# A recurrence in groups of 128 tokens: the block inverse on 32x32 tiles of TensorE, another order of VectorE's work, and two steps on GpSimd

## What is computed

```python
def step(S, inp):
    r_t, w_t, k_t, v_t, kk_t, a_t = inp
    sa = jnp.einsum('bhvk,bhk->bhv', S, -kk_t)
    S = (S * w_t[:, :, None, :]
         + sa[..., None] * (kk_t * a_t)[:, :, None, :]
         + v_t[..., None] * k_t[:, :, None, :])
    return S, jnp.einsum('bhvk,bhk->bhv', S, r_t)
_, o = lax.scan(step, S0, xs)
...
o = ((o - mean) * lax.rsqrt(var + GN_EPS)).reshape(B, T, W)
...
return (o * g.astype(jnp.float32)).astype(p.dtype)
```

## Time and profile before

| | us |
|---|---|
| median of 3 runs (lowest, highest) | 1324.94 (1324.16, 1328.39) |
| the profiled execution's own time | 1324.93 |
| its span, first to last instruction | 1323.0 |
| TensorE busy (share of the span) | 1275.8 (96%) |
| VectorE busy | 853.1 (64%) |
| ScalarE busy | 479.3 (36%) |
| GpSimd busy | 254.3 (19%) |
| mean granted TensorE clock | 0.994 of full speed |

### The profile page before, as it was taken

How to read it: one execution, slowest core, us unless ns; L and a number is a source line. 1 busy time by engine, 2 the same in 40 slices (tenths; PEclk the granted TensorE clock), 3 DMA queues, 4 the chain that set the end, 5 groups by cost and what they waited for, 6 DMA issues and landing times.

```text
span 1323.0 us, 18110 instructions
## 1 busy us (share of the span) xinstructions
PE 1275.8 (96%) x6973; PEld 1057.7 (80%) x6973; DVE 853.1 (64%) x1308; ACT 479.3 (36%) x847; POOL 254.3 (19%) x196
## 2 busy tenths in 40 slices
PE   7999999989899999999999999999999999999996
PEld 6888888655698888888878888888888888888885
DVE  6865623399778787744476656566777676546765
ACT  6100032488422232234363333333333334333334
POOL 0476600034300000000003331332233200000001
PEclk9999999999999999989999999999999999999998
DMA  5576532200322333333214123214544567766643
GB/s 222 173 246 232 207 121 92 104 2 17 80 71 71 75 103 94 115 123 127 80 48 127 52 93 96 83 62 159 175 141 162 191 222 293 250 210 209 210 140 135
DMA packets 117232, 179.05 MB, mean 135 GB/s; under 512 B 30368, under 2 KB 59040, under 8 KB 116896
## 3 DMA queue, kind: packets, MB, share of 16 engines
q1 hardware_dynamic: 117152, 177.96, 41.0%
HBM read 123.90 MB, written 53.49 MB: 134 GB/s over the span
## 4 chain that ended last, share of the span: by engine, by line
PE 88%; DVE 7%; issue 2%; DMA 2%; ACT 2%; POOL 0%; DVEq 0%; SPq 0%; ACTq 0%; POOLq 0%
PE bank L2317 28%; PE bank L369 21%; PE bank L2417 15%; PE bank L1400 4%; PE bank L474 2%; PE bank L383 2%; PE bank L1271 1%; PE bank L1527 1%; PE bank L1485 1%; PE bank L1479 1%; DVE scores L1178 1%; PE bank L992 1%; PE bank L1497 1%; PE bank L1514 1%; PE bank L1501 1%
## 5 line engine op out<-in xcount | busy, mean ns | idle before, releaser
L2317 PE MATMUL bank<-thi,ahi 128*128 128x512 f32 x320 | 124.5, 389 | 0.0
L2317 PE MATMUL bank<-tlo,ahi 128*128 128x512 f32 x320 | 124.5, 389 | 0.0
L2317 PE MATMUL bank<-thi,alo 128*128 128x512 f32 x320 | 124.5, 389 | 0.0
L2417 PE MATMUL bank<-ch,dwh 128*128 128x512 f32 x308 | 120.3, 391 | 0.6 <-DVE dwl L1995 0.6
L2417 PE MATMUL bank<-ch,dwl 128*128 128x512 f32 x308 | 119.9, 389 | 0.0
L2417 PE MATMUL bank<-cl,dwh 128*128 128x512 f32 x308 | 119.8, 389 | 0.0
L348 DVE TENSOR_TENSOR ring_wlo<-ring_raw,ring_whi 128x1024 fp32r<-128x1024 f32 x30 | 40.6, 1352 | 121.9 <-ACT ring_whi L342 121.9
L369 PE MATMUL bank<-hhi,ring_whi 128*128 128x512 f32 x288 | 114.4, 397 | 0.0
L369 PE MATMUL bank<-hhi,ring_wlo 128*128 128x512 f32 x288 | 112.2, 390 | 0.0
L369 PE MATMUL bank<-hlo,ring_whi 128*128 128x512 f32 x288 | 112.1, 389 | 0.0
L2317 PE MATMUL bank<-x1hi,ahi 128*128 128x512 f32 x240 | 93.4, 389 | 0.0
(11 more groups left out here) (336 smaller groups left out, 2862.2 us busy)
## 6 DMA issues: line engine op xcount, KB each, us to landing
hraw<-hid_scratch SPq DMA_DIRECT2D x12, 1024.0 KB, 5.7
hid_scratch<-hid SPq DMA_DIRECT2D x22, 512.0 KB, 6.1
hid_scratch<-rt SPq DMA_DIRECT2D x11, 1024.0 KB, 4.7
dwr<-down_sums SPq DMA_DIRECT2D x16, 704.0 KB, 4.2
ring_raw<-in_w_in SPq DMA_DIRECT2D x20, 512.0 KB, 4.3
raw_a<-in_w_gate_up SPq DMA_DIRECT2D x20, 512.0 KB, 4.4
raw_b<-in_w_gate_up SPq DMA_DIRECT2D x20, 512.0 KB, 5.2
dwr<-in_w_down SPq DMA_DIRECT2D x12, 704.0 KB, 4.1
```

The lines of the kernel that those rows point to most:

```text
L2317: mm = pe.matmul(b[:, :], w[:, k, :], m[:, k, :], start=opens and k == 0 and i == 0, stop=not (j, n) in parts and k == 3 and i == 2, skip_ ...
L2417: mm = pe.matmul(b[:, :], w[m % 2][:, k, :], a[:, k, :], start=opens and k == 0 and i == 0, stop=name not in PART2 and k == KF - 1 and i = ...
```

## The change

It touches the recurrence, and the end of stage 8.

- **Levels 1 and 2** become matmuls on 32x32 tiles of the array (`blocks_of`). Level 1 has 32 matmuls for `t1` (16 columns each), 32 for `y1` (32 columns) and 16 for `x1` (16 columns), which computes the change of `X` and takes the place of the transposes; level 2 has 16 for `t2` and 16 for `y2` (32 columns each). Those of `t1` and `y1` go through four tiles on the array's diagonal in turn, the others through two.
- **The tiles shrink**: `X` and `XT` hold 64 instead of 128 columns for each head, `Ts1` and `Ts2` hold 32. Each of the two loads in `scatter` becomes two loads of 64 partitions. `vtk` has two buffers, and its load moves ahead of `scatter`.
- **VectorE**: one multiplication (`first_corners`) and two additions (`first_updates`) are left of levels 1 and 2. `masked` b moves from the end of a group to the start of the next; `lanes` stands ahead of `prepare`; `Sn` stands ahead of `masked` k. The scaling of the mean goes into the instruction that makes `oc`, which now waits for the mix sum of the group before.
- **ScalarE** makes the copies of level 2 (`Ts2`, and two into `XT`), and copies `bt` and `kt` ahead of scaling `S`.
- **GpSimd** normalises (`on`) and adds to `mix`, except for the last group.
- **TensorE**: the product of the state for `R` stands first in a group, the products of `KB` stand between the steps of levels 1 and 2, and `bt` and `kt` around the close of the state. `busy` issues matmuls of 128x512 whose result is not used: four in group 0, three in group 7.
- **Stage 8**: the transposes of three quarters move to `k == 7`, and ScalarE squares those three quarters before the last one is there, in instructions of their own (`square_three`, then `square_last` on 128 columns).

The diff, cut. GpSimd and the copies in memory first:

```diff
-                sp.dma_start(X[:, :, :], bass.AP(d_i.tensor, P, [[2 * P, P], [8 * IMG2, H], [1, P]])).then_inc(s_xl, 16)
-                if t:
-                    C.result(sp, "U", t - 1)
-                sp.dma_start(XT[:, :, :], bass.AP(d_i.tensor, 0, [[2 * P, P], [8 * IMG2, H], [1, P]])).then_inc(s_xt, 16)
+                for m, o, done in ((X, P, s_xl), (XT, 0, s_xt)):
+                    if t and m is XT:
+                        C.result(sp, "U", t - 1)
+                    for q in range(2):
+                        sp.dma_start(m[q * HD:(q + 1) * HD, :, :],
+                                     bass.AP(d_i.tensor, o + q * (2 * P + 1) * HD, [[2 * P, HD], [8 * IMG2, H], [1, HD]])
+                                     ).then_inc(done, 16)
...
                     gather(t + 1)
+                    sp.wait_ge(s_vtk, 16 * t + 16)
+                    if t:
+                        C.result(sp, "S", t - 1)
+                    sp.dma_start(vtk_[(t + 1) % 2][:, :], v_dram[tok(t + 1), :]).then_inc(s_vtk, 16)
                     scatter(t + 1)
-                    C.result(sp, "S", t)
-                    sp.dma_start(vtk[:, :], v_dram[tok(t + 1), :]).then_inc(s_vtk, 16)
...
+                if t < NT - 1:
+                    pool.wait_ge(s_rstd, 2 * t + 2)
+                    pool.tensor_tensor(on[:, :, :], oc[:, :, :], rstd.unsqueeze(2).to_broadcast([P, H, HD]), ALU.mult
+                                       ).then_inc(s_on, 1)
+                    C.emptied(pool, "ot", t)
+                    pool.tensor_tensor(mix[:, 0:NP, tok(t)], oc[:, :, :].rearrange("p (a b) n -> p a (b n)", a=NP),
+                                       mix[:, 0:NP, tok(t)], ALU.add).then_inc(s_mix, 1)
```

TensorE's new functions, and the start of a group:

```diff
+            def blocks_of(b, count, lhs, rhs, groups):
+
+                n = len(groups) * H
+                for h in range(H):
+                    for g in groups:
+                        lo, ro = lhs(g, h), rhs(g, h)
+                        to = g[2]
+                        mm = pe.matmul(b[32 * to:32 * to + 32, h * count:(h + 1) * count] if len(ro.shape) == 2 else
+                                       b[32 * to:32 * to + 32, h * count:(h + 1) * count].rearrange("p (a w) -> p a w", a=2),
+                                       lo, ro, start=h == 0, stop=h == H - 1, skip_group_check=True)
...
+
+            FOUR = [(g, g % 2, g) for g in range(4)]
...
+                if n == 1:
+                    b = C.claim(pe, "t1", t)
+                    pe.wait_ge(s_xl, 32 * t + 32)
+                    C.done(blocks_of(b, 16, lambda g, h: NB[t % 2][rows(g[0]), h, 1, rows(g[0])],
+                                     lambda g, h: X[rows(g[0]), h, 32 * g[1]:32 * g[1] + 16], FOUR), "t1", t)
+                else:
+                    b = C.claim(pe, "t2", t)
+                    C.emptied(pe, "x1", t)
+                    C.done(blocks_of(b, 32, lambda g, h: NB[t % 2][rows(g[0]), h, 1, rows(g[2])],
+                                     lambda g, h: X[rows(g[0]), h, 0:32], [(0, 0, 1), (2, 0, 3)]), "t2", t)
...
+                C.emptied(pe, f"t{n}", t)
+                if n == 1:
+                    b = C.claim(pe, "y1", t)
+                    C.done(blocks_of(b, 32, lambda g, h: Ts1[rows(g[0]), h, :],
+                                     lambda g, h: XT[rows(g[0]), h, :].rearrange("p (a w) -> p a w", a=2)[:, :, 16:32], FOUR),
+                           "y1", t)
+                    b = C.claim(pe, "x1", t)
+                    C.done(blocks_of(b, 16, lambda g, h: XT[rows(g[0]), h, 0:32],
+                                     lambda g, h: Ts1[rows(g[0]), h, 0:16], [(0, 0, 0), (2, 0, 2)]), "x1", t)
+                else:
+                    C.emptied(pe, "y1", t)
+                    b = C.claim(pe, "y2", t)
+                    C.done(blocks_of(b, 32, lambda g, h: Ts2[rows(g[0]), h, :],
+                                     lambda g, h: XT[rows(g[0]), h, 32:64], [(1, 0, 0), (3, 0, 2)]), "y2", t)
+
+            def busy(b, n):
+                for _ in range(n):
+                    pe.matmul(b[:, :], ident, cst[:, 0:HALF], start=True, stop=True)
...
+                br = C.claim(pe, "R", t)
+                if t == 0:
+                    busy(br, 2)
+                else:
+                    pe.wait_ge(s_S, t)
+                of_state(br, alpha, True)
                 if t:
...
+                    corners(1, t)
                 pe.wait_ge(s_vtk, 16 * t + 16)
                 for g in range(4):
                     C.emptied(pe, f"k{g}", t)
...
+                products_of(br, 1, *range(H)).then_inc(s_r, 1)
...
-                              stop=False, skip_group_check=True)
+                if t == 0:
+                    corners(1, t)
+                    products_of(bo, 0, *range(4))
+                    busy(C.claim(pe, "S", t), 1)
+                pe.wait_ge(s_xt, 32 * t + 32)
+                updates(1, t)
+                if t == 0:
+                    busy(C.claim(pe, "S", t), 1)
+                else:
+                    products_of(bo, 0, *range(4))
+                corners(2, t)
+                products_of(bo, 0, *range(4, H))
+                if t:
+                    outputs(t - 1)
+                updates(2, t)
+                if t + 2 < NT:
+                    cumulative(pe, t + 2)
+                if more:
+                    of_state(bo, rho, False)
```

ScalarE and VectorE:

```diff
+            def last_updates(t):
+                b = C.result(act, "y2", t)[:, 0:32 * H].rearrange("p (h n) -> p h n", h=H)
+                act.activation(XT[0:32, :, 32:64], b[0:32, :, :], ACT.Copy)
+                C.read(act.activation(XT[64:96, :, 32:64], b[64:96, :, :], ACT.Copy), "y2", t)
...
-                keep_x("x1", t)
+                act.wait_ge(s_r, t + 1)
+                act.activation(rs_[low, :], bank[0][low, :], ACT.Copy).then_inc(s_rlow, 1)
...
+                    C.result(act, "S", t)
+                    if t + 2 < NT:
+                        keep("bt", t + 1, bt[:, :])
+                        keep("kt", t + 1, kt_[:, :])
                     C.emptied(act, "S", t)
...
+            def first_corners(t):
+                b = C.result(dve, "t1", t)[:, 0:16 * H].rearrange("p (h n) -> p h n", h=H)
+                C.read(dve.tensor_scalar(Ts1[:, :, 0:16], b, cst[:, C_PAIR + 2:C_PAIR + 3], None, ALU.mult), "t1", t)
+
+            def first_updates(t):
+                b = C.result(dve, "y1", t)[:, 0:32 * H].rearrange("p (h a n) -> p h a n", h=H, a=2)
+                v = XT.rearrange("p h (a n) -> p h a n", a=2)[:, :, :, 16:32]
+                c = C.result(dve, "x1", t)[:, 0:16 * H].rearrange("p (h n) -> p h n", h=H)
+                C.read(dve.tensor_tensor(X[:, :, 0:16], c, X[:, :, 0:16], ALU.add), "x1", t)
+                C.read(dve.tensor_tensor(v, b, v, ALU.add), "y1", t)
...
-                corners(1, t)
+                if not last:
+                    masked(dve, "b", NB[(t + 1) % 2], t + 1, 0, 1)
+                    if not t:
+                        masked(dve, "b", NB[1], 1, 2, 3)
+                first_corners(t)
+                if 0 < t < NT - 1:
+                    masked(dve, "b", NB[(t + 1) % 2], t + 1, 2, 3)
+                first_updates(t)
                 if t:
-                    normalise(t - 1)
-                updates(1, t)
-                if t:
-                    outputs(t - 1)
+                    gated(t - 1)
...
+                    lanes(t + 1)
                     if t + 2 < NT:
                         prepare(dve, t + 2)
-                    lanes(t + 1)
-                    masked(dve, "k", KB, t + 1, 0, 1)
```

Stage 8:

```diff
+                if first:
+                    pe.wait_ge(s_sq8, 12 + n + 1)
...
-                    if m == 4 * len(TURN) - 1 and k == KF - 2:
+                    if m == 4 * len(TURN) - 1 and k == 7:
                         by_tokens(pe, 0, 1, 0, 3)
...
+            def square_three(n):
+                act.wait_ge(s_part, len(parts) + 12 + n + 1)
+                act.activation(fin[:, n, HALF:HALF + 3 * P], D2.bank("f01", n)[:, 0:3 * P], ACT.Square,
+                               accum_out=st[:, 4, n:n + 1]).then_inc(s_sq8, 1)
...
+            def square_last(n):
+                b = D2.result(act, "f01", n)
+                act.activation(fin[:, n, HALF + 3 * P:D], b[:, 3 * P:HALF], ACT.Square, accum_out=st[:, 1, n:n + 1]
```

227 lines of the change are left out of this document (89 added, 138 removed).

## The result

The changed kernel takes 1316.99 us (median of 20 runs, 1312.22 to 1328.99) against 1326.12 (20 runs, 1324.16 to 1328.39): ratio 0.9939, 95% interval 0.9924 to 0.9954. It is faster, by 0.6%, where 2.6% were forecast: 1290 us, range 1285 to 1316. The profiled execution took 1315.93 us, 9.0 less than that of before; the forecast was 34.6 less. One execution is left out of all that follows: one of e16's four, which took 5130 us.

The account below looks back on a forecast made before the run. The prediction took TensorE to bound the groups, with the loop through `X` just under it. Savings of 25.6 us before the last group, 6.5 in it, 1.4 in first output products and 1.1 at the end made 34.6: 1290 us, range 1285 to 1316.

Parts of the forecast that it names:

- Small matmuls: Levels 1 and 2 on TensorE: 0.014 us a record on four tiles, 0.016 on two, 0.20 per tile-shape change.
- Group 0: First group of the recurrence: its first step was to take 23.6 us.
- so they cost nothing: Group 0: the state's product, `R` and the fillers run before `X` lands, so were to add no time.
- The loop beside it: The chain through `X`, once round per group: 23.8 us, just under TensorE's 24.3.
- From `t1` on: `Ts1` … `X` 4.1: 23.8 us: Sum of the loop: `Ts1` and masked b 3.4, n_scratch 3.2, `LA` 2.7, `lanes` 7.2, LM 3.2, `X` 4.1 us.
- The last group: Last group of the recurrence: 18.1 us from `t1` on against 24.6, 6.5 us saved.
- Part of that is the clock … The fillers stand in just those waits: Last group: TensorE was at 0.50 for 6.75 us after waits of 0.7 us, which three fillers were to fill.
- Hidden steps: GpSimd's two steps (1.7 us each) and ScalarE's copies of level 2 were to lie under other work.
- Stage 8: End of the kernel: six instructions taking 1.85 us on 512 columns were to take 0.8 on 128, 1.1 us less.
- a clock under 0.98 between 355 and 550 us: Sign of being wrong: TensorE's granted clock falls below 0.98 in that stretch of the recurrence.
- Slower clock: Rival, chance 0.06: 32-wide stretches pull TensorE to 1.2 GHz once a group, at 3.3 us each; 1316 us.
- The rival of the loop: Rival, chance 0.06: DMA and VectorE become the bound; `X` takes 5.5 us, the loop 25.2 us; 1296 us.

Follow-up runs that it names:

- e16: The kernel before, with two more reductions of 0.67 us on VectorE ahead of `Ts1` in groups 1 to 7: 1343.1 us.
- e17: e1 with the 2 MB load of x issued earlier, once `LA` of the last group has landed: 1306.1 us.
- e3: The changed kernel with `cumulative`, the exponentials and `prepare` moved ahead of level 2 and `lanes` on VectorE: 1342.4 us.
- e12: e10 without the four fillers of group 0: 1328.9 us.
- e1: The changed kernel with three fillers in the wait for `S` and four in the wait for `X` ahead of the last group: 1308.5 us.
- e9: e5 with the mean, `oc` and variance of the group before placed behind `Ts1` on VectorE: 1318.6 us.
- e5: The changed kernel with VectorE masking k 2,3 and all of b at the group's end, ahead of the mean: 1340.1 us.
- e6: The changes of e3 and e5 together, on the changed kernel: 1366.5 us.
- e7: e3 with two fillers in the wait for `X` of groups 1 to 6, and e1's seven ahead of the last group: 1316.4 us.
- e13: e10 with one filler in the wait for the normalised outputs in groups 1 to 6, and the last group's mean and `oc` ahead of its `Ts1`: 1312.4 us.
- e18: e13 with the 2 MB load of x issued earlier, once `LA` of the last group has landed: 1315.4 us.
- e11: e10 with the 64 records of `t1` issued twice in groups 1 to 6: 1340.3 us.
- e15: e1 with two fillers in the wait for masked k ahead of the b products in groups 1 to 6: 1318.2 us.
- e10: e9 with three fillers in the last group's wait for `S`, two in its wait for masked k, and its `R` products ahead of `t1`: 1319.1 us.
- e4: The changed kernel with n_scratch written by two DMAs of 256-byte rows instead of one of 512-byte rows: 1318.6 us.

## Why the prediction was wrong

By its own steps, on the profiled runs:

- **Small matmuls: right, and cheaper than said.** `t1`'s 64 records with the change of tile shape take 0.73 us (e17's timeline), 0.011 us a record, where 0.014 and 0.2 for the change were taken. TensorE's work in a group is 22.9 us (e3), against 23.8 predicted. One reading on the way was wrong: of two L992 records that span 0.34 us, the later one lasting 0.27 to 0.32, the row says that it starts at least 0.016 us after the first, not at most. That the number held is luck; the trace's single records start 0.013 to 0.014 us apart. By the Trainium skill, "TensorE: Matmul & The Clock Gate", section "Wait — 56ns, not 53.3ns?", start-to-start is never below about 25 ns. The traces do not agree for tiles in turn: 64 records would take 1.6 us.
- **Group 0: the fillers are not free.** The step "so they cost nothing" failed. They and the two products run after `X` has landed: 26.8 us from 354.8 to 381.6, not 23.6. 3.2 us. That they hold the clock (e12) the prediction did not say.
- **The loop beside it: the wrong loop.** The step "From `t1` on: `Ts1` … `X` 4.1: 23.8 us" followed `X` and left out what stands behind `lanes` on VectorE: `prepare`, `Sn`, masked k, mean, `oc`, the second masked k, the variance and only then masked b. That is 24.4 us at best, and 26.7 where n_scratch lands after 4.9 us instead of 3.4 and the clock falls for 3.4 us. Moving `prepare` behind `lanes` did not take it out of a loop, it moved it into another. Two terms were short as well: n_scratch, taken at 3.2 us, landed after 3.4 to 4.9, which no run explains, and the way through `X` took 24.9 us where e3 made it the bound. Groups 1 to 5 take 126.7 us, not 121.5; group 6 27.3, not 23.9: 8.6 us.
- **The last group: the clock.** "Part of that is the clock … The fillers stand in just those waits" failed. The waits that start the fall are new and stand ahead of the group, 3.2 us for `S` and 3.3 for `X`, since TensorE has nothing to prepare there: the same saving that the prediction counted. 31.2 us, not 18.1: 13.1 us. With these filled the term is close (18.9 in e1, 18.2 in e17, each with 1.4 us of wait for the output weights). The output products begin with 3.7 us at half clock, so the 1.4 us there were not saved but 0.5 more lost: 1.9 us.
- **Hidden steps: right.** `on` takes 1.04 us and the mix sum 1.26 on GpSimd, and neither they nor ScalarE's copies are waited for in the changed kernel. In e9, once TensorE was faster, `on` was 0.9 us late.
- **Stage 8: right.** From the last transposes to the end of ScalarE's work it is 4.90 us, not 5.94.

3.2 + 8.6 + 13.1 + 1.9 are 26.8 us. 34.6 less these are 7.8; 9.0 were measured; the other 1.2 us lie in the stretch ahead of stage 8's end, and no run says where. Of the prediction's own signs of being wrong one came in: a clock under 0.98 between 355 and 550 us (0.96 over the seven groups).

Of the rivals, "Slower clock" (0.06) named the right mechanism and, with its 1316 us, the time; it had the place wrong: it took 3.3 us lost in each group, and the trace has two falls of 3.4 us, four groups with none, and one fall of 41 us. That its 1316 us meets the measured time is luck. The rival of the loop (0.06) had the right kind of bound on the wrong path. Two rivals came true together, which none of the cases held.

The experiments say more than either. Every step meant to shorten the loop that left a wait of 1.7 to 2 us ahead of or among the narrow groups (e3, e5, e6) made the kernel slower, and fillers (e7, on e3) or another order on VectorE (e9, on e5) took 26 and 21 us off again. At 1.2 GHz the work is stretched, and in the changed kernel's groups the clock can stay there: 27.3 us with TensorE busy throughout (e1). The Trainium skill describes swings of the clock by waits for DMAs ("TensorE: Matmul & The Clock Gate", section "HAM oscillation — how this bites in real kernels"). The traces agree in that the falls stand at waits, but these are as short as 0.7 us (e13, e18), and most are not waits for a DMA of data.

Open: what share the narrow tiles have in starting a fall (e11 has longer waits for issue as well), and in how long it lasts; and whether other DMAs make the waits for instructions longer. The spread between runs of one kernel, up to 21 us (e7), goes with the mean clock, 0.980 to 0.992 in e1, and is larger than several of the differences above; only those over some 8 us are read as effects here.

## What to carry to other kernels

Where the traces show an engine's clock falling at its own waits, as TensorE's here, a saving that ends in idle time can cost more than it brings. Before removing work from TensorE ask what it will wait for next and what it runs right behind that wait: in one group of e16 a wait of 1.6 us with 128-wide matmuls behind it was followed by 3.4 us at half clock; in one of e5, with 32-wide groups behind it, a wait of 1.8 us by 13.7. When costing a loop, follow each in-order engine once round in its own order, not only the data.

## What the runs showed of the hardware

- 64 matmul records (fp32, 32x32 tiles, 16 columns) on four tiles of the array's diagonal in turn take 0.73 us, the change from full tiles among it (e17).
- A granted clock of 0.50 for 27.3 us while TensorE's busy share is 1.0 (e1), with no wait in it.
- 46 of 48 waits of TensorE with releaser "issue" end 1.2 to 1.55 us behind a 16 KB packet of the instruction queue; the longest, 2.4 us, is in e15.
- Matmuls whose result is not used can make a kernel faster: e7 over e3 by 26 us, e10 over e12 by 10 us.
- Two DMAs of 256-byte rows in place of one of 512-byte rows, the second issued 0.6 us behind the first: both halves of `X` have landed about 3.5 us after the first issue (2.9 each) instead of 4.1, those of n_scratch (e4) after 3.1 (2.5 each) instead of 3.4.
